# A transformer layer in one kernel: constant products ahead of the first sums, another order of scalings and modulations, and the value tile a block behind the gate latent

## What is computed

```python
def rmsnorm(x, w):
    xf = x.astype(jnp.float32)
    y = xf * lax.rsqrt(jnp.mean(xf * xf, axis=-1, keepdims=True) + EPS)
    return (y * w.astype(jnp.float32)).astype(x.dtype)

def modulate(x, w, shift, scale):
    return rmsnorm(x, w) * (1 + scale) + shift

def adaln(cvec, w_mod, b_mod, n):
    m = jax.nn.silu(cvec) @ w_mod[:, : n * D_MODEL] + b_mod[: n * D_MODEL]
    return jnp.split(m, n, axis=-1)
...
        h = modulate(x, norm1_w[l], sh1, sc1)
        proj = h @ w_in[l]
...
        x = mix_and_mlp(x, proj, o_lat, rows, g1, sh2, sc2, g2, norm2_w[l], gla_norm_w[l], conv_w[l],
                        pool_w[l], pool_scale[l], w_out[l], w_mlp1[l], w_mlp2[l])
    return rmsnorm(x, final_norm_w)
```

## Time and profile before

| | |
|---|---|
| median of 3 runs | 1192.86 us (1190.93 to 1196.22) |
| the profiled execution, its own time | 1193.7 us |
| its span, first to last instruction | 1191.9 us |
| PE busy | 1117.8 us, 94% of the span |
| DVE, ACT, POOL busy | 751.5, 455.2, 188.0 us |
| mean granted clock of TensorE | 0.979 of full speed |

### The profile page before, as it was taken

The page is one execution under the profiler, slowest core; times in us unless marked ns, Lnnn a source line. Parts: engine busy times, 40 slices in busy tenths (PEclk is TensorE's granted clock), DMA queues, the critical chain, the costliest instruction groups (busy, mean ns, idle before and its releaser), DMA issues.

```text
span 1191.9 us, 14125 instructions
## 1 busy us (share of the span) xinstructions
PE 1117.8 (94%) x5190; PEld 896.6 (75%) x5190; DVE 751.5 (63%) x977; ACT 455.2 (38%) x699; POOL 188.0 (16%) x116
## 2 busy tenths in 40 slices
PE   4899999789999999889999999999999999999995
PEld 1478877667878778668888888888888888888883
DVE  3777859744753786685845737548448457376485
ACT  5456425324543412255233243143252342332444
POOL 1100000120000354430210201201101203011023
PEclk9899999889999999989999999999999999999998
DMA  9423321010011374011201111210202111102013
GB/s 373 169 89 107 105 94 49 18 36 18 19 36 41 134 283 143 18 53 36 89 36 54 70 35 35 70 35 35 88 18 87 36 53 70 35 35 70 18 35 141
DMA packets 28437, 88.44 MB, mean 74 GB/s; under 512 B 2288, under 2 KB 3568, under 8 KB 27888
## 3 DMA queue, kind: packets, MB, share of 16 engines
q1 hardware_dynamic: 28400, 87.95, 20.8%
HBM read 83.74 MB, written 4.19 MB: 74 GB/s over the span
## 4 chain that ended last, share of the span: by engine, by line
PE 78%; DVE 10%; ACT 6%; issue 2%; DMA 2%; POOL 1%; SPq 0%; POOLq 0%; DVEq 0%; ACTq 0%
PE main L1053 28%; PE main L732 14%; PE main L1077 13%; PE sm L1077 7%; PE ob L1077 5%; DVE tst L1638 3%; PE main L947 2%; ACT tst L1215 2%; PE main L748 1%; DVE xg L1878 1%; DVE h_lo L1885 1%; DVE a_lo L1783 1%; PE ob L897 1%; PE ob L764 1%; DMA raw<-wstream 1%
## 5 line engine op out<-in xcount | busy, mean ns | idle before, releaser
L1077 PE MATMUL main<-tset,slot 128*128 128x512 f32 x672 | 157.9, 391 | 0.0
L1053 PE MATMUL main<-h_hi,w_hi 128*128 128x512 f32 x480 | 149.7, 393 | 1.3 <-DVE w_lo L1923 1.3
L1053 PE MATMUL main<-h_hi,w_lo 128*128 128x512 f32 x480 | 148.7, 391 | 0.0
L1053 PE MATMUL main<-h_lo,w_hi 128*128 128x512 f32 x480 | 148.4, 390 | 0.0
L1077 PEld LDWEIGHTS main<-tset,slot 128*128 128x128 f32 x672 | 125.6, 188 | 28.5 <-DVE X L1971 1.7
L732 PE MATMUL main<-a_hi,w_hi 128*128 128x512 f32 x376 | 127.0, 419 | 2.6 <-DVE a_lo L1783 2.6
L732 PE MATMUL main<-a_lo,w_hi 128*128 128x512 f32 x376 | 117.9, 395 | 0.0
L732 PE MATMUL main<-a_hi,w_lo 128*128 128x512 f32 x376 | 117.1, 393 | 0.0
L1425 ACT ACTIVATE hid<-main 128x512 f32<-128x512 f32 (+1 forms) x48 | 35.3, 735 | 189.9 <-PE main L1053 189.9
L1053 PEld LDWEIGHTS main<-h_hi,w_hi 128*128 128x128 f32 x480 | 90.1, 188 | 21.2 <-DVE w_lo L1923 1.7
L1053 PEld LDWEIGHTS main<-h_lo,w_hi 128*128 128x128 f32 x480 | 90.1, 188 | 20.6
(11 more groups left out here) (283 smaller groups left out, 1852.9 us busy)
## 6 DMA issues: line engine op xcount, KB each, us to landing
raw<-wstream SPq DMA_DIRECT2D x60, 512.0 KB, 3.3
raw<-wstream SPq DMA_DIRECT2D x16, 1024.0 KB, 5.2
wmod<-wm SPq DMA_DIRECT2D x4, 2048.0 KB, 23.4
mbuf<-wm SPq DMA_DIRECT2D x16, 512.0 KB, 3.7
mbuf_late<-wm SPq DMA_DIRECT2D x16, 512.0 KB, 4.8
xs<-xt SPq DMA_DIRECT2D x8, 512.0 KB, 9.2
X<-xt SPq DMA_DIRECT2D x2, 2048.0 KB, 11.1
out<-X SPq DMA_DIRECT2D x16, 256.0 KB, 3.0
```

The source lines that it names most:

```text
L1053: ins = pe.matmul(main[:, bank_pair, half * HALF:(half + 1) * HALF], w[:, slot, k, :], x[:, half * HALF:(half + 1) * HALF], start=begin, s ...
L1077: ins = pe.matmul(product_bank(s, acc, q), slot[:, w, q, kp, :], tset[j][:, kp, x, :], start=begins and kp == 0 and n == 0, stop=kp == 1 a ...
```

## The change

Four edits, all in the start.

1. `keep_busy`: PE issues 34 products of the ones with the 359 columns of `small` as soon as `small` is there, ahead of the first sum, and 12 more between the first and the second sum. They write a bank of `sm` that nobody reads before it is written anew.
2. The value tile: `first_products` is parted into `gate_part(k)` and `value_part(k)`; for blocks 0 and 1 the value part stands behind the rows of modulation 2 and 3, and from block 2 on value_part(k-1) follows gate_part(k). Only value_part(0) waits for the weight's parts.
3. The weight tile: its high part moves on ACT from ahead of the first `copy_rows` to behind the second one, its low part from POOL to DVE behind `low1(1)`.
4. DVE's order: scalings and modulations alternate. ACT's copies of rows 2 and 3 stand a block earlier.

```diff
+FILL = (34, 12)
...
-                if t == 0:
-                    pool.wait_ge(hi_made, 1)
-                    pool.tensor_tensor(w_lo[:, 0, :, :], raw[:, 0, :, :], w_hi[:, 0, :, :].bitcast(F32),
-                                       ALU.subtract).then_inc(split_done, 1)
...
+            def keep_busy(count):
+
+                for _ in range(count):
+                    pe.matmul(sm[:, 0, 0:NFIRST], ones, small[:, 0:NFIRST], start=True, stop=True)
+
+            pe.wait_ge(small_in_done, 16)
+            keep_busy(FILL[0])
             pe.wait_ge(c_ready, 1)
-            pe.wait_ge(small_in_done, 16)
...
                 ins = pe.matmul(ob[:, HALF:HALF + NC], ones, squares[:, N:NA], start=(n == 0), stop=(n == 2))
+                if n == 0:
+                    keep_busy(FILL[1])
             ins.then_inc(sums1_done, 1)
...
+            def value_part(k):
+
+                if k == 0:
+                    pe.wait_ge(split_done, 1)
+                ins = first_product_of(k, 1, slice(0, P), [(w_hi[:, 0, k, :], a_hi, c_hi), (w_hi[:, 0, k, :], a_lo, c_lo),
+                                                           (w_lo[:, 0, k, :], a_hi, c_hi)])
+                if k == KT - 1:
                     ins.then_inc(tile_done, 1)
...
             pe.wait_ge(wg_split, 1)
-            pe.wait_ge(split_done, 1)
-            first_products(0)
+            gate_part(0)
             modulation_rows(2)
+            value_part(0)
             modulation_turned(2)
-            first_products(1)
+            gate_part(1)
             modulation_rows(3)
+            value_part(1)
             modulation_turned(3)
             for k in range(2, KT):
-                first_products(k)
+                gate_part(k)
+                if k >= 3:
+                    value_part(k - 1)
+            value_part(KT - 1)
             gate_products(0)
...
-            weight_high(0)
             copy_rows(0)
...
-                if k in (0, 2, 3):
-                    copy_rows((1, None, 2, 3)[k])
+                if k == 0:
+                    copy_rows(1)
+                    weight_high(0)
+                if k in (1, 2):
+                    copy_rows(k + 1)
...
             scale1(0)
+            modulation(0)
             scale1(1)
-            modulation(0)
             low1(0)
             modulation(1)
             scale1(2)
+            low1(1)
+            weight_low(0)
             scale1(3)
-            low1(1)
             low1(2)
-            low1(3)
             modulation(2)
             scale1(4)
+            low1(3)
+            modulation(3)
             scale1(5)
             low1(4)
-            modulation(3)
+            scale1(6)
             low1(5)
-            scale1(6)
             scale1(7)
             low1(6)
```

More of the change, by code:

```diff
@@ L938, in gate_products, with first_product_of @@
                 ins.then_inc(tile_done, 1)
[L941 to L945, removed]
+            def first_product_of(k, m, rows, parts):
+                for n, (w, x, c) in enumerate(parts):
+                    begin, end = k == 0 and n == 0, k == KT - 1 and n == len(parts) - 1
                     for half in range(2):
                         pe.matmul(main[rows, m, half * HALF:(half + 1) * HALF], w,
[L948 to L961, removed]
@@ new lines, in first_product_of, with gate_part @@
+                                  x[:, k, half * HALF:(half + 1) * HALF], start=begin, stop=end)
+                    ins = pe.matmul(ob[rows, m * HALF:m * HALF + NC], w, c[:, k, :], start=begin, stop=end)
+                return ins
+            def gate_part(k):
+                pe.wait_ge(h1_lo, k + 1)
+                wide, narrow = slice(0, 4 * RANK), slice(0, 2 * RANK)
+                both, hi = wg_parts[:, k, :], wg_parts[:, k, 0:2 * RANK]
+                if k < KT - 1:
+                    first_product_of(k, 0, wide, [(both, a_hi, c_hi)])
+                    for half in range(2):
+                        pe.matmul(main[narrow, 0, half * HALF:(half + 1) * HALF], hi,
+                                  a_lo[:, k, half * HALF:(half + 1) * HALF], start=False, stop=False)
+                    pe.matmul(ob[narrow, 0:NC], hi, c_lo[:, k, :], start=False, stop=False)
+                else:
+                    for half in range(2):
+                        pe.matmul(main[narrow, 0, half * HALF:(half + 1) * HALF], hi,
+                                  a_lo[:, k, half * HALF:(half + 1) * HALF], start=False, stop=False)
+                    pe.matmul(ob[narrow, 0:NC], hi, c_lo[:, k, :], start=False, stop=False)
+                    first_product_of(k, 0, wide, [(both, a_hi, c_hi)]).then_inc(tile_done, 1)
```

## The result

| | before | changed |
|---|---|---|
| median of 4 runs | 1191.89 us | 1203.26 us |
| ratio, 95% interval | | 1.0093, 1.0071 to 1.0115 |
| profiled execution, its own time | 1193.7 us | 1200.9 us |
| span | 1191.9 us | 1199.1 us |
| sums taken by ACT (T) | 25.74 | 39.54 |

Slower by 0.93%, some 11 us; 1205 was forecast. The page's head, for the earlier trace rows: PE is busy for 23 us more, for the same work of the layer.

The account below looks back on a forecast made before the run. The start's chain through PE to the value tile V0 was taken to set the end: +14.6 us until the sums are done (T), -2.5 from T to V0, together +12.1, so 1205 us, range 1200 to 1210.

Parts of the forecast that it names:

- What a constant product costs, 0.60 us: On PE ahead of and between the sums: 359 columns at 1.69 ns each, 0.60 us, 1.2 us at the low clock.
- T at 40.3: Sums done at 3.25 + 27.6 (46 constant products) + 6.45 (three sums) + 3.0 (PE's cold start at low clock), 14.6 us later.
- T + 11.0 for block 0: PE starts block 0 11.0 us after the sums are done, against T + 14.5 before.
- The new wait at value part 0 for w_lo, 2.0 us: PE waits 2.0 us at value part 0 until DVE finishes the weight tile's low part at T + 16.9.
- a fall of the clock that costs 1.1 us: PE's clock falls ahead of the turned products and returns after some 6 us of work: V0 at T + 47.0, not T + 45.9.
- The stall at gate part 4, 1.3 us: PE runs dry 1.3 us before low 4 comes at T + 31.8, behind ACT's row 3 copy and DVE's queue.
- Nothing changes behind V0: After ACT fetches the finished value tile V0 the rest is only shifted: what V0 loses or gains, the end does.
- The rule of the Trainium skill: Warm-up matmuls ahead of the sums: by the rule T comes 3.1 us sooner, by the operands' arrival only 0.8 us.
- constants hidden: Rival, 10%: a constant product takes 0.30 us, the first 34 end just behind acc1, T = 26.5, 1191 us.
- a gain of 4.5 us: Rival, 3%: constants cost nothing and the clock never falls, T = 24.9, V0 at 70.8, 1188.4 us.
- constants that don't raise the clock: Rival, 3%: all 46 constant products and the sums run at 1.2 GHz, T 45.6 us late, time near 1236 us.
- a smaller overrun: Rival, 4%: V0 at T + 42 and T at its lower bound 38.8, +5.5 us, 1198.4 us.

Follow-up runs that it names:

- 180 columns: Changed kernel with its 34 + 12 constant products cut to 180 columns instead of 359: 1191.09 us, ratio 0.9990 to the kernel before.
- weight tile as before: Changed kernel without constant products, weight tile's high part on ACT ahead of the first row copy, low part on POOL: 1193.22 us, ratio 1.0008.
- orders as before: Changed kernel without constant products, DVE's scalings and modulations and ACT's row copies in the old order: 1189.03 us, ratio 0.9979.
- 17 + 3: Changed kernel with 17 constant products ahead of the first sum and 3 behind it instead of 34 and 12: 1188.36 us, ratio 0.9960.
- clock held: Changed kernel with 17 and 3 constant products, ACT's row 3 copy and DVE's modulation 3 later, four more constant products in PE's gaps: 1188.60 us, ratio 0.9962.
- 17 + 3 and both orders mended: Changed kernel with 17 and 3 constant products, ACT's row 3 copy behind block 3, DVE's scaling 5 and low 4 ahead of modulation 3: 1187.38 us, ratio 0.9950.

## Why the prediction was right

The range, the sign and the mechanism held: the constant products cost their own time and more than the other edits win. That 1205 came so close owes something to luck. At V0 the forecast was +12.1 us and the trace shows +9.4, while the runs give +11.1; the runs' interval, 8.5 to 13.7 us, holds both. By its steps:

- *What a constant product costs, 0.60 us.* Right: 12 of them took 7.24 us, 0.603 each. The rival that a product might cost 0.30 us fell; at 180 columns it does, and the whole change then comes out even, 0.999, close to the price of 0.34 us at which the prediction put the turn.
- *T at 40.3.* Measured 39.54. The term that was off is the cold start: the first 34 took 22.66 us, 2.3 more than 34 x 0.60, not 3.0. It isn't the same each time: in the kernel before with the same constants they took 23.59, 3.2 more.
- *T + 11.0 for block 0.* The gate part began at 50.13, T + 10.6 (before T + 14.5). Right, also in the causes: with the weight tile as before it began at T + 12.9, with the orders as before at T + 11.9. DVE's two scalings took 1.49 us each; before, the second of them took 3.65, from 30.3, while POOL wrote w_lo from 29.78 to 32.57.
- *The new wait at value part 0 for w_lo, 2.0 us, and a fall of the clock that costs 1.1 us.* The two were added up, and that was the step that was wrong. The clock did fall, but while PE would have waited for w_lo anyway: value part 0 began at T + 16.2, and at T + 16.1 in the three kernels whose clock held up to there. So the fall cost about 0.1 us, not 1.1, and V0 came at T + 45.2 instead of 47.0; the rest of that difference is DVE, which had w_lo ready at T + 16.0, so that value part 0 began 0.7 us sooner than I had added up. The 13 us that I gave the fall in the kernel before were a misreading as well: the granted clock was 1.00 there from 35.5 to 38.5, between two falls.
- *The stall at gate part 4, 1.3 us, from ACT's and DVE's queues.* Measured 1.08; with ACT's copy moved it is 0.28 and with DVE's order mended too it is gone, which shows the cause.
- *Nothing changes behind V0.* Right at first: the first `zsb` product on PE comes at 86.63, 9.4 us later than before, and in both 1.9 us behind ACT's fetch of V0. The span is only 7.2 us longer; where the other 2.2 us went is told below. The code there is the same in both kernels.
- *The rule of the Trainium skill* (TensorE: Matmul & The Clock Gate, "Why this matters for your kernels"), to warm up with matmuls: the trace agrees that constant products raise the clock, since behind them the first sum's wide products took 1.72 us, and 3.75 before. It is worth little here, between nothing and 0.8 us, since data arrives at the sums later than the warm-up can help.

None of the four rivals came: constants hidden, a gain of 4.5 us, constants that don't raise the clock, a smaller overrun.

## What to carry to other kernels

Work put on an engine to fill its idle time needs a length, in time and not in instructions: count it in the columns and passes of the nearest product in the trace, and end it before the operand that is waited for; here 17 fitted where 34 were put, and even those won at most 0.8 us. A wait that moves has to be weighed with what it hides, since a slow clock ahead of a wait costs only what exceeds the wait. Edits that are measured together can hide one another: three of these four won 4.5 us between T and V0, the fourth lost 14 ahead of T.

## What the runs showed that I had not expected

From the fetch of V0 to the end the code is the same in all 13 kernels, yet it takes 1114.3 us in one profile and 1122.2 in another (1116.6 in the kernel before, 1114.4 in the changed one). So an effect of a microsecond is read from T and V0, not from a span. One place where such profiles part can be seen. The products of the heads' outputs (`ob<-a_sum,vtok`) start, first to last, in the kernel before and in the changed one (instructions of this line: duration in ns min/median/max, first and last start in us):

```profile
L894 PE MATMUL ob<-a_sum,vtok x64: 271/275/552, 237.5 to 353.0; 128*128 128x128 f32 x64
```

```profile
L900 PE MATMUL ob<-a_sum,vtok x64: 271/276/527, 247.6 to 359.4; 128*128 128x128 f32 x64
```

115.5 and 111.8 us for the same instructions. In all 13 profiles that length is either 111.7 to 111.8 (the changed kernel, 17 + 3, 180 columns, orders as before, clock held) or 115.3 to 115.5 (the other eight), and nothing lies between. Windows of the kernel before, and then of the changed one at the same place of the program:

```profile
245.50:248.00 2.50, 0.77 (x4) 0.80 (x4) 1.55 (x2) 0.00 (x0) 2.42 (x2) 0.80 0.53 198
248.00:254.00 6.00, 6.00 (x26) 5.69 (x26) 0.00 (x0) 1.02 (x1) 1.95 (x2) 0.52 0.01 3
```

```profile
256.00:262.00 6.00, 5.27 (x34) 4.52 (x35) 0.59 (x1) 1.09 (x2) 3.37 (x3) 1.00 0.09 38
```

PE waits for DVE just ahead of these windows, with little to do. Before, the clock fell to 1.2 GHz and stayed there for about 6 us of full work; in the changed kernel it stayed at 2.4 GHz. These 3.7 us are more than the 2.2 us by which the span's growth falls short of the 9.4 at V0: by this stretch's first start the changed kernel was 10.1 us behind, by its last 6.4, and at the end 7.2, so that 0.7 us were lost ahead of the stretch and 0.8 behind it. Whether the same falls make the runs of one kernel differ was not shown, since each kernel has one profile; but their times do go with the granted clock: of the kernel with 17 + 3 and both orders mended, the run of 1182.57 us had a mean of 0.984 and that of 1190.42 had 0.978. Why the clock falls there in one profile and not in the next is not settled, as the code of the stretch is the same. Whether constant products in that later gap would hold it was not tried.
